# Banded attention in an encoder kernel: the distance-times-slope tiles move into the read of the scores, and the groups are written out

## The reference

```python
q = q.reshape(B, nb, BLK, A_KV_HEADS, A_GROUP, A_HEAD_DIM) * (A_HEAD_DIM ** -0.5)
dist = jnp.abs(qpos[:, :, :, None] - kpos[:, :, None, :]).astype(jnp.float32)
scores = jnp.einsum('bnqkgd,bnskd->bnkgqs', q, kb).astype(jnp.float32)
scores = scores - slopes[None, None, :, :, None, None] * dist[:, :, None, None]
scores = jnp.where(mask[None, :, None, None], scores, NEG)
p = jax.nn.softmax(jnp.concatenate([scores, sink_col], axis=-1), axis=-1)[..., :-1]
```

## Time and profile before

| what | value |
|---|---|
| runs | 1268.41 us median, 1266.66 to 1269.77 (3 runs) |
| profiled execution | 1270.9 us, span 1268.9 us |
| mean granted clock of TensorE | 0.985 of full |
| busy, TensorE matmuls | 1200.9 us |
| busy, VectorE | 632.2 us |
| busy, GpSimd | 421.5 us |
| busy, ScalarE | 371.3 us |
| banded attention, four groups | from 58.68 to 202 us of the span |

### The profile page before, as it was taken

One profiled execution on the slowest core, in us unless ns is written; L12 is line 12 of the kernel. 1 busy time (PEld: TensorE's weight loads), 2 busy tenths in 40 slices (PEclk: granted clock), 3 DMA queues, 4 the chain that ended last, 5 costly groups with the idle time before them and its releaser, 6 DMA issues.

```text
span 1268.9 us, 19233 instructions
## 1 busy us (share of the span) xinstructions
PE 1200.9 (95%) x5796; PEld 996.9 (79%) x5796; DVE 632.2 (50%) x1051; ACT 371.3 (29%) x723; POOL 421.5 (33%) x467
## 2 busy tenths in 40 slices
PE   6988899999999999999989899999999999999996
PEld 5777787878888888888967677778788888888885
DVE  5667665443433534445476767745433332343432
ACT  4267662222210011111265666632222200111101
POOL 3355543333321332234142313215333321333342
PEclk8899999999999999999999999999999999999998
DMA  6211012323333233332201001013323432333331
GB/s 158 67 34 33 17 34 67 95 87 99 103 105 91 83 99 98 98 113 88 76 17 36 19 17 33 1 34 116 100 83 99 118 92 83 91 97 99 111 88 66
DMA packets 176471, 96.61 MB, mean 76 GB/s; under 512 B 8752, under 2 KB 173104, under 8 KB 176432
## 3 DMA queue, kind: packets, MB, share of 16 engines
q1 hardware_dynamic: 176432, 96.12, 26.1%
HBM read 94.01 MB, written 2.10 MB: 76 GB/s over the span
## 4 chain that ended last, share of the span: by engine, by line
PE 80%; DVE 7%; issue 5%; ACT 3%; POOL 3%; DMA 1%; DVEq 0%; ACTq 0%; POOLq 0%; SPq 0%
PE bank L986 25%; PE bank L988 25%; PE bank L987 25%; PE bank L1428 2%; POOL w_hi L441 1%; PE bank L1125 1%; DVE w_lo L1510 1%; DVE stat L2034 1%; POOL bias L515 1%; DVE bpt_lo L2039 1%; DMA x_n<-in_x 1%; DVE apt_lo L1696 0%; ACT s_b L917 0%; DVE k_dup L1616 0%; DVE w_lo L1527 0%
## 5 line engine op out<-in xcount | busy, mean ns | idle before, releaser
L1510 DVE TENSOR_TENSOR w_lo<-w_raw,w_hi 128x1024 fp32r<-128x1024 f32 (+2 forms) x151 | 202.5, 1341 | 299.0 <-POOL w_hi L441 298.9
L441 POOL TENSOR_SCALAR w_hi<-w_raw 128x1024 fp32r<-128x1024 f32 (+3 forms) x159 | 183.5, 1155 | 422.0 <-PE bank L988 411.1
L986 PE MATMUL bank<-x_hi,w_lo 128*128 128x512 f32 x784 | 309.5, 395 | 10.1 <-DVE w_lo L1510 7.9
L987 PE MATMUL bank<-x_lo,w_hi 128*128 128x512 f32 x784 | 307.8, 393 | 0.0
L988 PE MATMUL bank<-x_hi,w_hi 128*128 128x512 f32 x784 | 307.7, 393 | 0.0
L986 PEld LDWEIGHTS bank<-x_hi,w_lo 128*128 128x128 f32 x784 | 148.6, 189 | 42.5 <-DVE w_lo L1510 5.8
L988 PEld LDWEIGHTS bank<-x_hi,w_hi 128*128 128x128 f32 x784 | 148.7, 190 | 31.6
L987 PEld LDWEIGHTS bank<-x_lo,w_hi 128*128 128x128 f32 x784 | 148.7, 190 | 29.7
L986 PE MATMUL bank<-f_hi,w_lo 128*128 128x512 f32 x352 | 137.8, 391 | 1.0 <-DVE f_lo L1806 1.0
L988 PE MATMUL bank<-f_hi,w_hi 128*128 128x512 f32 x352 | 137.0, 389 | 0.0
L987 PE MATMUL bank<-f_lo,w_hi 128*128 128x512 f32 x352 | 137.0, 389 | 0.0
(11 more groups left out here) (222 smaller groups left out, 1916.2 us busy)
## 6 DMA issues: line engine op xcount, KB each, us to landing
w_raw<-in_ffn_w_gu SPq DMA_DIRECT2D x88, 512.0 KB, 3.8
w_raw<-in_ffn_w_down SPq DMA_DIRECT2D x32, 704.0 KB, 4.4
w_raw<-in_a_w_qkv SPq DMA_DIRECT2D x12, 512.0 KB, 3.7
w_raw<-in_a_w_o SPq DMA_DIRECT2D x8, 512.0 KB, 3.6
w_raw<-in_b_w_o SPq DMA_DIRECT2D x8, 512.0 KB, 3.7
w_raw<-in_b_w_in SPq DMA_DIRECT2D x4, 672.0 KB, 4.1
w_raw<-in_b_w_uq SPq DMA_DIRECT2D x4, 576.0 KB, 4.0
x_n<-in_x SPq DMA_DIRECT2D x4, 512.0 KB, 5.4
```

Source lines behind the costliest of these rows:

```text
L441: pool.tensor_scalar(split_part(w_hi, s, cols, kv), raw_part(s, cols, kv), 1.0, 1.0, ALU.mult, ALU.mult) \
L986: pe.matmul(o, ll, rh, start=start, stop=False)
L987: pe.matmul(o, lh, rl, start=False, stop=False)
L1510: dve.tensor_tensor(split_part(w_lo, s, cols, kv), raw_part(s, cols, kv), f(split_part(w_hi, s, cols, kv)), ALU.subtract) \
```

## The change

The queries are divided by the slope of their head: a_q_out multiplies by a column of q_gain, (1/8)/slope, in place of the constant 1/8 (one column holds two heads, 64 partitions each, as q_tmp does). read_scores then computes s_a = -slope x (near + bank), with near itself as input and the slope as a constant of the instruction. The tiles bias and par and the semaphores around them go; GpSimd's and ScalarE's making of the bias goes with them. The negated sinks are kept in one tile minus_sink. What the wait for a bias tile had implied, read_scores now waits for itself: for near, once, and, in the first two query blocks of a group, for the previous group's transposes out of the same slot of s_a. The loops over groups 0 to 2 are written out on all four engines, so the slope is known where the instruction is made. SyncE's loop stays.

```diff
@@ -94,6 +94,9 @@
 ROUND = 12582912.0
+SLOPES = [float(np.float32(2.0 ** (-8.0 * (i + 1) / HEADS))) for i in range(HEADS)]
+
+
 TAB_STEPS = 21
 LRS_KV, LRS_Q = 6, 7
@@ -154,8 +157,8 @@
         gains = tile("gains", [P, 4, KD, 1])
         g_q = tile("g_q", [P, QL // P])
         g_kv = tile("g_kv", [P, KVL // P])
-        par_all = tile("par_all", [P, GROUPS, 2 * HG])
-        par = tile("par", [P, 2 * HG])
+        minus_sink = tile("minus_sink", [P, HEADS])
+        q_gain = tile("q_gain", [P, HEADS // 2])
         sink_in = tile("sink_in", [P, HEADS])
         stat = tile("stat", [P, 3, 8])
         sums_n = tile("sums_n", [P, 8])
...
@@ -460,9 +461,6 @@
             pool.wait_ge(pool_consts, 1)
             pool.affine_select(out=ident[:], in_=ident[:], compare_op=ALU.not_equal, fill=1.0, base=0,
                                pattern=[[-1, P]], channel_multiplier=1).then_inc(pool_consts, 1)
-            for i in range(HEADS):
-                slope = float(np.float32(2.0 ** (-8.0 * (i + 1) / HEADS)))
-                pool.memset(par_all[:, i // HG, i % HG:i % HG + 1], slope).then_inc(pool_consts, 1)
             w_split_hi(0, 0, W_COLS)
             w_split_hi(0, 1, W_COLS)
@@ -494,34 +492,18 @@
             pool.wait_ge(near_p, 3 * NT)
-            pool.wait_ge(pool_consts, 2 + HEADS)
+            pool.wait_ge(pool_consts, 2)
             pool.wait_ge(vec_consts, 6)
             def a_group(g, last=False):
-
-                wait(pool, s_free, S_A + 16 * g)
-                pool.tensor_copy(par[:], par_all[:, g, :]).then_inc(par_ready, 1)
-                wait(pool, par_ready, g + 1)
                 wait(pool, pt_done, T_A + A_TG * g)
                 for b in range(2):
-                    pool.tensor_copy(s_a[:, b, :, 0:1], par[:, HG:2 * HG].unsqueeze(2)).then_inc(sinkcol_ready, 1)
-
-                def make_bias(u):
-                    nk = A_KB[u // HG][1]
-                    if u >= 2:
-
-                        wait(pool, s_free, S_A + 16 * g + u - 1)
-                    pool.tensor_scalar(bias[:, u % 2, 0:nk * P], near[:, u // HG, 0:nk * P],
-                                       par[:, u % HG:u % HG + 1], 1.0, ALU.mult, ALU.mult).then_inc(bias_ready, 1)
-
-                make_bias(0)
+                    pool.tensor_copy(s_a[:, b, :, 0:1], minus_sink[:, g * HG:(g + 1) * HG].unsqueeze(2)).then_inc(sinkcol_ready, 1)
+
                 for u in range(16):
                     n, hd = u // HG, u % HG
                     nk = A_KB[n][1]
-                    if u + 2 < 16 and u % 2 == 0:
-                        make_bias(u + 2)
-
                     wait(pool, rsum_ready, 16 * g + u + 1)
                     view = s_a[:, n % 2, hd, 1:1 + nk * P]
                     pool.tensor_scalar(view, view, stat[:, 2, u % 8:u % 8 + 1], 1.0, ALU.mult, ALU.mult) \
@@ -532,7 +514,7 @@
                         w_split_hi(C_Q // 2 + 2 + g, 0, W_COLS)
             w_split_hi(C_Q // 2 + 1, 0, W_COLS)
-            with pool.Fori(0, GROUPS - 1) as g:
+            for g in range(GROUPS - 1):
                 a_group(g)
             a_group(GROUPS - 1, last=True)
@@ -730,17 +712,6 @@
                     act.activation(view, view, ACT.Exp, scale=-1.0, bias=stat[:, 0, u % 8:u % 8 + 1],
                                    accum_out=stat[:, 1, u % 8:u % 8 + 1]).then_inc(exp_ready, 1)
-                def odd_bias(u):
-                    nk = A_KB[u // HG][1]
-                    if u == 1:
-
-                        wait(act, par_ready, g + 1)
-                    else:
-
-                        wait(act, s_free, S_A + 16 * g + u - 1)
-                    act.activation(bias[:, 1, 0:nk * P], near[:, u // HG, 0:nk * P], ACT.Copy,
-                                   scale=par[:, u % HG:u % HG + 1]).then_inc(bias_odd_ready, 1)
-
                 def pt_hi(n, i):
                     unit = T_A + A_T0[n] + i
                     wait(act, pt_done, unit + A_TG * g + 1)
@@ -751,23 +722,15 @@
                     act.activation(ot_hi_q[:, g, :, n, :], banks[5][:, 0:2 * P].rearrange("p (a q) -> p a q", a=2),
                                    ACT.Copy).then_inc(o_hi_ready, 1)
-                odd_bias(1)
-                expo(0)
-                expo(1)
-                odd_bias(3)
-                expo(2)
-                expo(3)
-                odd_bias(5)
+                for u in range(4):
+                    expo(u)
                 for n in range(NT):
                     if n < 3:
                         expo(4 * n + 4)
                         expo(4 * n + 5)
-                        odd_bias(4 * n + 7)
                         expo(4 * n + 6)
                         pt_hi(n, 0)
                         expo(4 * n + 7)
-                        if n < 2:
-                            odd_bias(4 * n + 9)
                         pt_hi(n, 1)
                         if n:
                             o_hi(n - 1)
@@ -787,7 +750,7 @@
                     a_v_hi(g + 1)
             ot_hi_q = ot_hi[:].rearrange("p (g a) (n q) -> p g a n q", a=2, n=NT)
-            with act.Fori(0, GROUPS - 1) as g:
+            for g in range(GROUPS - 1):
                 a_group(g, False)
             a_group(GROUPS - 1, True)
...
@@ -1570,6 +1533,10 @@
             for t in (kp_hi, kp_lo, av_hi, av_lo):
                 dve.memset(f(t[:]), 0.0).then_inc(vec_consts, 1)
+            for i in range(HEADS):
+                dve.memset(q_gain[i % 2 * HD:(i % 2 + 1) * HD, i // 2:i // 2 + 1], HD ** -0.5 / SLOPES[i]) \
+                    .then_inc(q_gain_ready, 1)
+
             def read_x(pos):
                 dve.wait_ge(pt_done, pos + 1)
                 dve.tensor_copy(h[:, K_ORDER[pos], :], banks[K_ORDER[pos]][:]).then_inc(pt_free, 2)
@@ -1604,8 +1571,9 @@
             take_rs_t(norms[0])
             w_split_lo(C_Q // 2, 0, W_COLS)
             dve.wait_ge(small_in, 8 * 16)
-            dve.tensor_scalar(par_all[:, :, HG:], sink_in[:].rearrange("p (g h) -> p g h", g=GROUPS), -1.0, None,
-                              ALU.mult).then_inc(vec_consts, 1)
+            dve.tensor_scalar(minus_sink[:], sink_in[:], -1.0, None, ALU.mult).then_inc(vec_consts, 1)
+            dve.wait_ge(vec_consts, 6)
+            dve.wait_ge(q_gain_ready, HEADS)
             for m in range(2):
@@ -1650,7 +1618,8 @@
                 wait(dve, w_used, C_Q + 2 * g + i + 1)
                 if not (first and i == 0):
                     wait(dve, q_ready, 2 * g + i)
-                dve.scalar_tensor_tensor(q_tmp[:], banks[6 + i][:], HD ** -0.5, rs_t[:], ALU.mult, ALU.mult) \
+                dve.scalar_tensor_tensor(q_tmp[:], banks[6 + i][:], q_gain[:, 2 * g + i:2 * g + i + 1], rs_t[:],
+                                         ALU.mult, ALU.mult) \
                     .then_inc(proj_free, 1)
             def a_q_lo(g, i):
@@ -1678,16 +1647,17 @@
                     n, hd = u // HG, u % HG
                     w = A_KB[n][1] * P
-                    if u % 2:
-                        wait(dve, bias_odd_ready, 8 * g + u // 2 + 1)
-                    else:
-                        wait(dve, bias_ready, 8 * g + u // 2 + 1)
                     wait(dve, s_done, 16 * g + u + 1)
+                    if g == 0 and u == 0:
+                        dve.wait_ge(near_p, 3 * NT)
                     if n >= 2:
                         wait(dve, pt_done, T_A + A_TG * g + A_T0[n - 1])
-                    dve.tensor_tensor_reduce(s_a[:, n % 2, hd, 1:1 + w], bias[:, u % 2, 0:w], banks[u % 3][:, 0:w],
-                                             -1.0, par[:, HG + hd:HG + hd + 1], ALU.add, ALU.min,
+                    elif g:
+                        dve.wait_ge(pt_done, T_A + A_TG * (g - 1) + (A_T0 + [A_TG])[n + 3])
+                    dve.tensor_tensor_reduce(s_a[:, n % 2, hd, 1:1 + w], near[:, n, 0:w], banks[u % 3][:, 0:w],
+                                             -SLOPES[4 * g + hd], minus_sink[:, 4 * g + hd:4 * g + hd + 1],
+                                             ALU.add, ALU.min,
                                              stat[:, 0, u % 8:u % 8 + 1]).then_inc(s_free, 1)
                 def pt_lo(n, i):
...
```

## The result

The changed kernel took 1250.09 us (median of four runs, 1248.54 to 1250.38) against 1268.72 for the kernel before; the ratio is 0.9851, 95% interval 0.9838 to 0.9865. Measured again beside the experiments it took 1250.70 against 1267.20, ratio 0.9883, 0.9852 to 0.9913 (the recorded ratios are not quotients of the medians, which here would be 0.9870). The profiled execution took 1250.18 us, span 1248.4, mean granted clock 0.990.

The account below looks back on a forecast made before the run. TensorE's waits for read_scores, held by bias tiles, were taken as the bound; group savings of 18.8 us less 0.1 for query scale and 0.1 for setup gave 18.6, so 1250 us, own range 1245.5 to 1254, reaching to 1257.5 with (a).

Parts of the forecast that it names:

- What bounds the kernel: Attention groups: TensorE waits 16.3 us for read_scores, which waits for bias tiles from GpSimd (10.7 us) and ScalarE (3.3).
- The replay of the second group: Second attention group replayed with VectorE free of the bias: score 11 due at 105.0 against 109.00, group 30.6 us.
- The 1.2 us of kept waits: Per group: 0.2 at score 15, 0.3 at block 2's transposes, 0.2 at its values, 0.5 for VectorE slips.
- the forecast wait at the transposes of block 2: In each group, TensorE's transposes of n = 2 were to wait 0.3 us behind apt_lo.
- The loops written out: Attention groups: computed waits and nops go, bounded at some 0.4 us a group; longer code costed at zero.
- The table load: ScalarE's 1.28 us load at each loop entry: two of three go, the first stays; inside the sum.
- The last group: Fourth attention group: 32.6 us against 35.02, keeping two waits unrelated to the bias, 0.76 and 0.97 us.
- The clock: Half-clock dips in groups one and three, priced at 0.8 us in the third, counted as gone with the stalls.
- The query scale: A column in place of the constant 1/8 costs 0.05 us each; two of eight on TensorE's path, 0.1 us.
- (a): Rival: VectorE's own loop takes the bias's place in the groups, losing 2 us more each; 1258 us, chance 0.14.
- (b): Rival: the longer written-out code stalls the engines in code fetch, making it slower; 1279 us with seven stops, chance 0.03.
- (c): Rival: next to nothing gained, as other dependences bind alike or half clock takes it back; 1267 us, chance 0.04.

Follow-up runs that it names:

- four slots: Kernel before, loops kept, with four slots for the bias tile in place of two: 1259.62 us, ratio 0.9922.
- the copy ahead: Changed kernel plus ScalarE's table load moved into setup, and for query blocks 1 and 2 pt_hi(n, 0) copied before exponent 4n + 6: 1247.24 us, ratio 0.9837.
- the filled kernel: Kernel before with 11 unused 512-column matmuls put in TensorE's setup wait ahead of the groups: 1265.87 us, ratio 0.9988.

## Why the prediction was right, and where it was not

- *What bounds the kernel*: right. TensorE's waits for the reads went from 16.3 to 1.4 us, with four slots to 7.4; making the tiles unread costs nothing that shows.
- *The replay of the second group*: right in its total, 30.82 us against 30.6, and to 0.1 us at score 11. The 1.2 us of kept waits were 1.4, but lay elsewhere: 0.6 at the third transposes of block 1, behind ScalarE's copy, where I had next to nothing; the forecast wait at the transposes of block 2 did not show. The replay had followed VectorE's and TensorE's order and not ScalarE's, whose exponent waits for a read with the copy queued behind it. The weight split took 1.61 us and not the 1.3 of the replay, but began sooner: it ended 8.73 us after the first score, where the replay had 8.66.
- *The loops written out*: the total was right, the parts were not. The replay took the last group's constant waits for all groups, so their effect was in it, but I put it at 0.4 us a group as a bound. Alone it is 2.8 us in the second group, and 3.6 us of attention when it comes last.
- *The table load*: this step failed. The prediction let one load stay, "now before an exponent whose input comes at the same time", and so took it as hidden. The load was issued only once the exponent's wait was over, and the first group paid 0.95 us for it. The next exponent starts at 59.93, 1.29 us after the load: no further cost of the switch shows. The first group's miss is 1.5 us, 32.44 against 30.9. Beside the load, 0.2 is what the second group missed as well, and the rest the second query block, for which 0.3 us had been allowed where it took 0.7. The other two loads went, as forecast.
- *The last group*: 33.14 us against 32.6. Its two own waits stayed, 0.60 and 0.97 us for 0.76 and 0.97 forecast; the copy's wait, which the forecast had not, is there too, and with the copy ahead the attention behind the last group's first score is 0.7 us shorter (34.62 to 33.92).
- *The clock*: the half-clock stretches in groups one and three are gone in both profiles of the changed kernel, which the groups' lengths carry. The 0.8 us a stretch was about right (0.7 and 0.7 in these groups by the filled kernel). But the first group's 1.6 us over the second were not the clock alone: without a stretch it still took 36.26. In the setup I had counted on the same clock before and after; from 47 to 57 us it was 0.66 in one profile and 1.00 in the other. Runs with the old setup reached the early first score too, so this was chance of the execution as far as the runs show. Without those 3.2 us and the 1.0 of the rest the profiled gain would be 16.3 us, 1252 by the median before, inside the range, and 2 us over the forecast. The closeness of 1250.1 to 1250 is partly luck.
- *The query scale*: 0.05 us was forecast, and L1621 takes 750 ns at the median against 692, 0.06. The read itself kept its time with another constant and near as input.
- *Rivals*: (a) did not happen, the reads wait for TensorE only. (b) did not: TensorE's weight loads waited for nothing shown 16.2 us in 10 places of the whole run instead of 16.8 in 11, and the instruction queue moved 24 packets instead of 21. The Trainium skill's page "Runtime: NRT & Kernel Launch" (Instruction fetch mechanics), which the prediction sets beside (b), ties its stall to a taken branch whose target lies outside the two pages then held, a condition that the prediction left out; whether TensorE's loop was such a case no run here shows, so the gapless loop end does not test it. (c) did not.

## What to carry to other kernels

A tile that only scales a constant by a number per head could be taken out of the chain here by scaling the other operand, although the engines that made it were half idle: count what the reader waits for, not what the maker works. With the loops kept, two more slots gave four fifths of what leaving the tile out gave. Of the loops, that of VectorE, the engine that alternates short instructions with waits, gave most: 1.6 us of the second group by itself, the other three together some 0.7. That is the one to try first.

## What the runs showed that I had not expected

- On VectorE a reciprocal and the read behind it stood 0.28 us apart in the kernel before and 0.07 in the changed one; it was 0.07 also with computed waits, once the bias had four slots or was gone.
- ScalarE's table load (1.28 us) came after the wait of the instruction that needs it, so it added itself to the chain; the same load at 43.12 us, in the setup, cost nothing that shows, and the attention was 1.0 us shorter.
- After the same 2.7 us of TensorE idleness at 47 to 50 us the granted clock from 47 to 57 us was 0.66 in one execution and 1.00 in others. In 21 runs of the kernel before the mean granted clock of a run and its time go together: 0.982 at 1269.9 to 1270.8 us, 0.989 and 0.990 at 1264.1 to 1265.9; the slowest, 1271.55, has 0.985. The spread of 7 us is more than several of the effects measured here, which is why the attention's length was used beside the time. Whether the change makes the setup's half clock rarer is open.
